# A two-block transformer kernel on one core: the delta rule's first inverse moved ahead of the roundings, transposes put beside weight slabs, other banks for the Fourier step, first blocks of two feed-forward loops reordered

## The reference

```
# first block:  h += [ssd | windowed attention] @ w_out
u = conv3(rms(h) @ w_up);  h = h + (silu(g_ff) * u_ff) @ w_down        # D_FF = 5632
h = h + sigmoid(rms(h) @ w_ple_gate) * pe
# second block
q, k, v, z, f, scal, gates = split(rms(x) @ w_in_2)
qkv = silu(conv5(q, k, v));  q, k = l2_norm(q) / sqrt(128), l2_norm(k)  # 8 heads of 128
# gated delta rule, forward and backward in time, chunks of 64 tokens:
a_mat = I + strict_lower(beta * k k^T * decay);  u, w = solve(a_mat, [v*beta, k*beta*exp(gc)])
# then per chunk: v_new = u - w S; o = q_dec S + (q k^T * decay) v_new; S = S*g_last + k_dec^T v_new
y_a = (rms(o) * g_head * silu(z)) @ w_dn_up
y_f = real(fft2(f over tokens and 128 channels)) @ w_fourier
x = x + (sigmoid(gates_a) * y_a + sigmoid(gates_f) * y_f) @ w_o
x = x + relu(rms(x) @ w_mlp_up)**2 @ w_mlp_down                         # D_FF_2 = 8192
out = rms(x)
```

## Time and profile before

| | |
|---|---|
| median of 3 runs | 3107.39 us |
| the profiled execution, its own time | 3112.39 us |
| its span, first to last instruction | 3110.6 us |
| PE busy | 3022.4 us (97%) |
| DVE, ACT, POOL busy | 2001.6, 1406.7, 331.9 us |
| mean granted TensorE clock | 0.991 |

### The profile page before, as it was taken

The page is one execution under the profiler, slowest core; times in us unless marked ns, Lnnn a source line. Parts: engine busy times, 40 slices in busy tenths (PEclk is TensorE's granted clock), DMA queues, the critical chain, the costliest instruction groups (busy, mean ns, idle before and its releaser), DMA issues.

```text
span 3110.6 us, 43069 instructions
## 1 busy us (share of the span) xinstructions
PE 3022.4 (97%) x14543; PEld 2491.6 (80%) x14543; DVE 2001.6 (64%) x2655; ACT 1406.7 (45%) x1764; POOL 331.9 (11%) x306
## 2 busy tenths in 40 slices
PE   8999999999999999999999999999999999999997
PEld 7878678887888888887888877778777888888886
DVE  5755766656666777667578656665555666666665
ACT  5444434444444444445554533333544444444443
POOL 0004960000000000000000244323000000000000
PEclk9999999999999999999999999999999999999999
DMA  6555333356555555553565523332565655565554
GB/s 216 176 183 165 126 122 122 113 193 207 189 188 184 187 189 187 190 189 129 184 233 172 169 96 108 108 114 95 189 215 177 196 189 189 182 195 189 189 182 135
DMA packets 145704, 525.77 MB, mean 169 GB/s; under 512 B 16416, under 2 KB 17184, under 8 KB 144864
## 3 DMA queue, kind: packets, MB, share of 16 engines
q1 hardware_dynamic: 140416, 504.25, 49.4%
q0 software_dynamic: 1600, 12.04, 1.0%
q10 hardware_dynamic: 3616, 8.52, 0.7%
HBM read 516.36 MB, written 8.39 MB: 169 GB/s over the span
## 4 chain that ended last, share of the span: by engine, by line
PE 68%; issue 25%; POOL 3%; DVE 2%; ACT 1%; DMA 1%; DVEq 0%; SPq 0%; POOLq 0%; ACTq 0%
PE bank L1956 19%; PE bank L1958 19%; PE bank L1957 19%; PE bank L2346 1%; PE bank L2338 1%; PE bank L2054 1%; PE bank L1981 1%; ACT w_hi L728 1%; DVE w_lo L1225 1%; PE bank L2458 1%; PE bank L2356 0%; PE bank L2207 0%; PE bank L2181 0%; POOL xs L569 0%; PE bank L2250 0%
## 5 line engine op out<-in xcount | busy, mean ns | idle before, releaser
L1225 DVE TENSOR_TENSOR w_lo<-w_raw,w_hi 128x1024 fp32r<-128x1024 f32 x952 | 1187.7, 1258 | 841.8 <-ACT w_hi L728 839.5
L728 ACT CAST w_hi<-w_raw 128x1024 fp32r<-128x1024 f32 x952 | 998.9, 1052 | 1403.5 <-PE bank L1958 1373.1
L1956 PE MATMUL bank<-w_hi,a_hi 128*128 128x512 f32 x2816 | 1124.2, 399 | 3.4 <-DVE a_lo L1231 2.7
L1958 PE MATMUL bank<-w_hi,a_lo 128*128 128x512 f32 x2816 | 1100.2, 391 | 0.0
L1957 PE MATMUL bank<-w_lo,a_hi 128*128 128x512 f32 x2816 | 1099.7, 391 | 0.0
L1956 PEld LDWEIGHTS bank<-w_hi,a_hi 128*128 128x128 f32 x2816 | 531.1, 189 | 120.2 <-issue 15.1
L1958 PEld LDWEIGHTS bank<-w_hi,a_lo 128*128 128x128 f32 x2816 | 530.3, 188 | 113.2
L1957 PEld LDWEIGHTS bank<-w_lo,a_hi 128*128 128x128 f32 x2816 | 531.3, 189 | 109.0 <-issue 4.1
L531 POOL TENSOR_TENSOR rstd<-rstd,neg_half 128x2 f32<-128x2 f32 x7 | 5.5, 785 | 1885.6 <-DVE rstd L1254 1885.6
L1956 PE MATMUL bank<-w_hi,m_hi 128*128 128x512 f32 x512 | 200.3, 391 | 5.1 <-DVE m_lo L1902 5.1
L1957 PE MATMUL bank<-w_lo,m_hi 128*128 128x512 f32 x512 | 200.1, 391 | 0.0
(11 more groups left out here) (387 smaller groups left out, 2574.1 us busy)
## 6 DMA issues: line engine op xcount, KB each, us to landing
w_raw<-weights SPq DMA_DIRECT2D x952, 512.0 KB, 4.2
gate<-gate_st ACTq DMA_DIRECT2D x8, 512.0 KB, 3.7
h<-gate ACTq DMA_DIRECT2D x8, 512.0 KB, 5.0
gain<-gains POOLq DMA_DIRECT2D x3, 1024.0 KB, 7.8
h<-x_tok SPq DMA_DIRECT2D x4, 512.0 KB, 10.9
w_proj_sb<-w_proj POOLq DMA_DIRECT2D x1, 2048.0 KB, 9.8
h_rest<-h POOLq DMA_DIRECT2D x1, 2048.0 KB, 13.9
h<-h_rest POOLq DMA_DIRECT2D x1, 2048.0 KB, 9.2
```

What stands on the lines that cost most here:

```text
L728: nc.scalar.copy(w_hi[:, s, :], w_raw[:, s, :]).then_inc(hi_ready, 1)
L1225: V.tensor_tensor(w_lo[:, s, :], w_raw[:, s, :], w_hi[:, s, :].bitcast(F32), ALU.subtract).then_inc(lo_ready, 1)
L1956: T.matmul(psum[t][:], left_hi[:, ts], wh, start=first, stop=False)
L1958: last = T.matmul(psum[t][:], left_lo[:, ts], wh, start=False, stop=final)
```

## The change

1. **Delta turn.** DVE forms `m` and the first inverse of both heads before it takes the first rounding of the turn (`split(q + 1, 0, 1)`), not behind it. PE transposes the first inverse of head 0 behind two gate slabs, not three, then one slab, head 1, one slab. ACT copies `r` of both heads before the exponentials `eT` and `qd` of either, with one rounding ahead of each copy.
2. **q and k transposed beside slabs.** The eight pieces stand ahead of slabs 4 to 7 of the last z chunk, two each; ACT and DVE read them out between the roundings of the first gate quad; the exponentials of the decays and DVE's product with beta move up by two roundings. The two heads swap banks (head 0 has banks 5 to 7), POOL no longer waits for pairs 0 and 1, and PE waits for pair 1 only ahead of head 1.
3. **Fourier banks.** The Fourier products use banks 5, 2 (first) and 7, 4 (second) and no longer wait for the last outputs of the delta rule.
4. **Up loop and mixed product.** The loop is written out on PE, ACT and DVE; its chunks use pairs 0 and 1; tiles of `mix` are transposed between slabs of the next chunk, and the last two at slab 3 of the first `w_o` chunk. The gates are stored unscaled and scaled inside the sigmoid.
5. **First blocks.** In both feed-forward loops the first block is written out, and its transposes stand behind the first slab of the next up chunk.

The diff, cut to its core:

```diff
-                self.x, self.bank = x, bank[2 + 3 * x:5 + 3 * x]
+                self.x, self.bank = x, (bank[5:8], bank[2:5])[x]
 POOL
-            for p in range(2):
-                pool.wait_ge(pair_free[p], 2 * (U_MIX + 1))
 ACT
-            split(q + 3)
+            split(q + 3, 0, 2)
             act.wait_ge(gc_mm, 1)
             ...
-            split(Q_MIX, 0, 3)
+            split(q + 3, 2, 4)
+            split(Q_MIX, 0, 1)
+            qkT_evac(0)
+            qkT_evac(2)
+            split(Q_MIX, 1, 2)
+            qkT_evac(4)
+            split(Q_MIX, 2, 3)
+            qkT_evac(6)
             z_evac(1)
             split(Q_MIX, 3, 4)
...
-                    scaled(gate_st[:, t], pair[0][t][:], N_MIX2, t).then_inc(pair_free[0], 1)
+                    nc.scalar.copy(gate_st[:, t], pair[0][t][:]).then_inc(pair_free[0], 1)
...
-                split(q + 1, 0, 2)
                 for hd in heads:
+                    split(q + 1, hd.x, hd.x + 1)
                     act.wait_ge(dn_rT, hd.of(i))
                     nc.scalar.copy(flat(hd.r), hd.bank[2][:]).then_inc(dn_r0, 1)
+                for hd in heads:
                     act.wait_ge(dn_diff, hd.of(i, 2, 1))
...
-            with act.Fori(0, D // NC) as n:
+            for n in range(DC):
                 ...
+                if n:
+                    rounded_operand(TR_WO2, 2 * (n - 1), 2 * n)
                 ...
-            rounded_operand(TR_WO2)
-            projected_operand(Q_WO2, U_WO2, xn_m, TR_MLP, C_MLP)
+            projected_operand(Q_WO2, U_WO2, xn_m, TR_MLP, C_MLP, own=TR_WO2)
 DVE
-            split(Q_Z2 + 3)
+            split(Q_Z2 + 3, 0, 2)
             dve.wait_ge(gc_exp, 1)
             ...
+            split(Q_Z2 + 3, 2, 4)
+            qkT_evac(1)
+            split(Q_MIX, 0, 1)
+            qkT_evac(3)
             ...
+            qkT_evac(7)
+            split(Q_MIX, 3, 4)
...
-                split(q + 1, 0, 1)
                 for hd in heads:
                     dve.wait_ge(dn_kk, hd.of(i))
                     ...
-                split(q + 1, 1, 2)
+                split(q + 1, 0, 1)
                 for hd in heads:
                     differences(hd, hd.eT, ALU.min)
-                split(q + 1, 2, 4)
+                split(q + 1, 1, 4)
...
-            rest_of_operand(TR_WO2)
             dve.wait_ge(h_moved, 3 * 16)
-            project_into_h(Q_WO2, TR_MLP, C_MLP, N_MLP)
+            project_into_h(Q_WO2, TR_MLP, C_MLP, N_MLP, own=TR_WO2)
 PE
-            ff_channels(U_FF + 1)
-            with pe.Fori(0, N_FF - 1) as j:
+            ff_block(0, between={1: lambda: ff_channels(U_FF + 1)})
+            with pe.Fori(1, N_FF - 1) as j:
+                ff_block(j)
...
-            chunk(Q_Z2 + 2, 1, U_Z2, a_hi, a_lo)
+            chunk(Q_Z2 + 2, 1, U_Z2, a_hi, a_lo,
+                  between={4: lambda: qk_turned(0, 1), 5: lambda: qk_turned(2, 3), 6: lambda: qk_turned(4, 5), 7: lambda: qk_turned(6, 7)})
...
                 for hd in heads:
+                    if hd.x == 1:
+                        pe.wait_ge(pair_free[1], 2 * (U_MIX + 1))
                     pe.wait_ge(dn_rows, hd.of(i))
...
-                for n in range(3):
+                for n in range(2):
                     gate_slab(n)
                 for hd in heads:
                     ...
-                    if hd.x == 0:
-                        gate_slab(3)
+                    gate_slab(2 + hd.x)
...
-            pe.wait_ge(dn_free, DNH + 2)
-                            last = T.matmul(bank[4 + g % 2][:, c * SEQ:(c + 1) * SEQ], fr[:, t, g * P:(g + 1) * P], dft_t[:, c, t],
+                            last = T.matmul(heads[g % 2].bank[0][:, c * SEQ:(c + 1) * SEQ], fr[:, t, g * P:(g + 1) * P], dft_t[:, c, t],
...
-                chunk(q, 2, V_MIX + n, fr_hi, fr_lo, DNH)
-                chunk(q + 1, 3, V_MIX + n, y_hi, y_lo, DNH)
+                chunk(q, 0, U_UP + n, fr_hi, fr_lo, DNH,
+                      between={2 + j: lambda j=j: operand_tiles(TR_WO2, mix, mix_chunk, 2 * (n - 1) + j) for j in range(2)} if n else None)
+                chunk(q + 1, 1, U_UP + n, y_hi, y_lo, DNH)
+            late_chunk(TR_WO2, mix_chunk, Q_WO2, 0, U_WO2, src=mix)
...
+            mlp_block(0, between={1: first_channels})
+            with pe.Fori(1, N_FF2 - 1) as j:
+                mlp_block(j)
```

More of the change, by code:

```diff
@@ L1308, in project_into_h @@
                     if c < DC - 1:
-                        split(q + 1)
+                        split(q + 1, 0, 3)
+                        if own is not None and c == 0:
+                            rest_of_operand(own, 6)
+                        split(q + 1, 3, 4)
                         split(q + 2, 0, QUAD - 1)
@@ L2235, in _, with ff_block @@
             chunk(Q_FF + 2, 1, U_FF, a_hi, a_lo)
-            ff_channels(U_FF + 1)
-            with pe.Fori(0, N_FF - 1) as j:
+            def ff_block(j, between=None):
                 q, use = Q_FF + 4 + 6 * j, U_FF + 1 + 3 * j
-                chunk(q, 0, use, a_hi, a_lo)
+                chunk(q, 0, use, a_hi, a_lo, between=between)
                 chunk(q + 2, 1, use, a_hi, a_lo)
@@ L2501, in mlp_channels, with first_channels, mlp_block @@
                 to_channels(m_stage, 0, 6).then_inc(ff_t, 1)
-            pe.wait_ge(pair_free[0], 2 * (U_MLP + 2))
-            mlp_channels()
-            with pe.Fori(0, N_FF2 - 1) as j:
+            def first_channels():
+                pe.wait_ge(pair_free[0], 2 * (U_MLP + 2))
+                mlp_channels()
+            def mlp_block(j, between=None):
                 q = Q_MLP + 2 + 4 * j
-                chunk(q, 2, V_MLP + j, a_hi, a_lo)
+                chunk(q, 2, V_MLP + j, a_hi, a_lo, between=between)
                 pe.wait_ge(ff_lo, N_FF + 2 * j + 2)
```

106 lines of the change are left out of this document (59 added, 47 removed).

## The result

The changed kernel takes **3080.12 us** (median of 4 runs, 3079.68 to 3080.55); the kernel before, on the same chip, 3107.14 us (4 runs, 3104.39 to 3108.72). The ratio is 0.9915 with a 95% interval of 0.9902 to 0.9927: 27.0 us faster. Forecast were 3074 us in a range from 3062 to 3087. The profiled execution of the changed kernel took 3079.98 us, span 3078.2; forecast for it was 3079.2.

A forecast was written before the change was run, and what follows sets the result against it. PE was taken as the bound, busy 3022.4 of 3110.6 us, leaving its holes and half clock to win. Terms 4.4 + 4.2 + 5.9 + 14.5 + 2.5 + 1.7 = 33.2 us gave 3079.2 profiled, 3074 us for runs, range 3062 to 3087.

The forecast's parts named there:

- The turn: Delta turn, four times: PE's holes of 0.4 and 2.3 us go; 14.5 us gained in all, bounds 10 to 21.
- the return: Delta turn: POOL's late products and masks delay the second level, so 1.5 of 5.3 us per turn are lost again.
- First blocks: First blocks of feed-forward and last loop: a slab covers the wait ahead of the transposes; 4.4 and 4.2 us gained.
- q and k: Last z chunk to first gate slab: 5.9 us gained despite new waits of 1.4 and 0.9 us; bounds 2.5 to 8.2.
- Fourier: Fourier: first two groups start without waiting for last outputs; 2.5 us gained, new hole of 1.7 us, bounds 0.8 to 4.2.
- the last of the sum: Whole kernel: profile forecast 3079.2 us, lowered because the median lies 5.0 us under the profiled execution, giving 3074 us.
- the other six tiles moved, at no cost of their own: Up loop and `w_o`: six transposed tiles leave the start of `w_o` and were taken to cost nothing where they go.
- up loop and `w_o`: Loop end to fifth `w_o` slab: 1.7 us gained despite 3.3 us wait for `h` and 1.7 us half clock.
- The first: Rival: the turn's stall comes back on POOL and DVE, 2.0 us won per turn, 3081 us; chance 0.20.
- The second: Rival: nothing new is late; turns win all 5 us, `h` lands under cover or clock holds, 3064 us; chance 0.13.
- The third: Rival: PE starves on instructions where loops were written out, a quarter lost there, 3118 us; chance 0.03.
- the fourth: Rival: no change; gains of single places are given back at the next wait for a transfer, 3107 us; chance 0.02.

The follow-up runs named there:

- before's first profile: The kernel before, unchanged: the profiled execution on which the forecast was made; span 3110.6 us.
- experiment 7: Changed kernel with POOL's two products of head 1 in each turn moved behind the masks of the second level; 3077.24 us (one run).
- experiments 2 and 3: On the kernel before: 2, the turn's new order on DVE and PE without ACT's part, 3088.01 us; 3, ACT's part alone, 3109.84 us.
- before's second profile: The kernel before, unchanged, profiled once more; 3105.80 us, span 3103.8.
- experiment 5: Changed kernel with the mixed product's transposes back behind the up loop, all at the start of `w_o`; 3080.06 us (one run).
- experiment 11: Changed kernel with later `h` wait, POOL's products reordered, decay rows ahead of POOL's q and k wait, ACT's first `f_half` ahead of its squares; 3070.66 us.
- experiments 5 to 8 and 11: Changed kernel variants: 5, 7, 11 as listed here; 6, DVE's wait for `h` later, 3076.13 us; 8, first decay rows and ACT's first `f_half` earlier, 3077.56 us.
- experiment 3: The kernel before with only ACT's new order in the turn: `r` of both heads copied ahead of the exponentials; 3109.84 us, ratio 1.0013.

## Why the prediction came out as it did

**The turn** came out at 14.3 us of before's first profile where 14.5 were forecast. Two small errors cancel in it: with the return taken away (experiment 7) a turn takes 83.1 us, so 5.0 us were to be had (88.1 less 83.1), not 5.3, and 1.15 of them returned, not 1.5. The experiments say which part does it: DVE's earlier inverses with PE's new order. The sentence that ACT copies `r` of head 1 only behind the exponentials described the stall but not its cause; that edit alone is worth nothing (experiments 2 and 3).

**First blocks, q and k, Fourier** were right against the profile they were read from: 4.35 and 4.1 us against 4.4 and 4.2, 5.7 against 5.9, 2.9 against 2.5. Part of that is half clock that the same code often doesn't get. The feed-forward takes 13.33 us in five of the six profiles that have its old code, the z chunk's stretch 33.6 in four of six, and Fourier 33.92 to 33.96 in four of seven (35.4 to 35.6 in the other three). Against those executions the gains are 2.7, 2.0 and 1.3 us. Fourier's edits were not run alone.

**The step that failed first is the last of the sum**: "The median of the runs is 5.0 us lower, 3107.39, so the runs should show" 3074 us. I carried the 5 us over as if they lay outside the touched places. More than half of what sets the first profile apart from the second lies inside: 3.7 us of half clock behind the z chunk and 1.6 at the feed-forward, in that one execution, and I had already counted both as gains of the change. Without them the sum is 27.9 us, that is 3079.5 us, and 27.0 were measured. That this comes so close is partly chance, since it leaves out what the next step got wrong, the half clock not foreseen, and Fourier's share; the touched places gave 25.6 us between before's second profile and the changed kernel's, and where the other 1.4 us between the medians lie is open.

**The forecast for the profile**, 3079.2 against 3079.98, was met by luck: the touched places gave 3.7 us less than forecast, and 2.9 us in its favour lay in untouched code, 1.05 ahead of the first slab and most of the rest between slabs 98 and 130 and at slab 448, where the half clock moves about as well.

**The step that failed second** is "the other six tiles moved, at no cost of their own". The 18.45 us from the loop's end to the fifth slab contained those six tiles, and I subtracted them there without adding them to the loop, where they cost 6 x 0.47 = 2.8 us (experiment 5). The transfer itself came 0.7 us earlier than worked out, so up loop and `w_o` together lost 0.3 us in the first profile instead of gaining 1.7. What was right is the wait that takes the cover's place and the half clock behind it. The reason given for that half clock, that both holes of over 3.1 us were followed by it, holds in before's first profile only: behind the feed-forward's hole of 3.20 us the clock stayed full in the five other profiles with that code, behind the last loop's of 3.11 it fell in all six.

**Not foreseen**: the half clock at the start of the up loop, -1.6 us in one of two profiles.

**The rivals.** The first was right in kind: the stall returns on POOL and DVE, but with 1.0 to 1.15 us per turn and not 3. Its time, 3081 us, is nearer to the 3080 measured than the forecast's 3074, but that doesn't speak for it: it allows the turns 8 us, and they gave 14.3. The second, nothing new is late, is what experiment 11 builds, and it gave 3071 us. The third and the fourth fell: no hole in the written-out loops, and the gains of single places were not given back at a transfer, but for the one wait for `h` that the forecast had.

## What to carry to other kernels

Before a profile's half-clock stretches are counted as the gain of an edit, ask whether the median contains them: where a profiled execution lies above the median, its surplus may sit at the very hole that the change removes. A second profile of the same kernel shows it. Price a moved instruction at both ends. When a reordering uncovers a wait, look at what stands queued behind it on the same engine and whether it needs what is waited for; here one line moved was worth 4.3 us, and the order of POOL's products 4.6.

## What the runs showed of the hardware

- A DVE product of 128x32 elements (L1741) took 3.54 us beside a POOL product of 3.61 us and ended with it; the copy of the same size just ahead of it took 0.19, and the same product in the kernel before, where no POOL product stood beside it (L1723), took 0.18. PE's wait was thus put down to DVE; by these rows it was POOL's product that set its end. The Trainium skill (SBUF — State Buffer, "Who interferes with whom") says that the loser of the shared ports waits for the whole instruction of the other; this row agrees, and so do the turn's roundings at 2.20 us beside products at 2.26, where a rounding ahead of them takes 1.21 and the first product 1.30.
- The same code with the same holes ran at half clock in one execution and at full clock in the next: 37.29 and 33.60 us for one stretch of before, 7.19 and 5.57 us for two slabs of the changed kernel. In the profiles of experiments 5 to 8 and 11 the second came out as 7.17 once and as 5.57 to 5.59 four times. The length of the hole alone doesn't tell: at the start of the up loop 2.19 us in the kernel before was followed by full clock in all seven profiles with that code, 1.88 us in the changed kernel and its variants by half clock in two of five.
- A hole of 2.78 us that took the place of one of 2.33 in each turn, with the half clock behind all four, made an edit that removes a wait slower than none (1.0013, experiment 3).
